# Moving three of the six h-splits one or two steps later in the gate groups of a fused attention and SwiGLU layer

## The reference, cut to what matters

```python
    x = x + jnp.concatenate([o_a, o_b], axis=-1) @ w_out[layer]
    h = rms_norm(x, norm_ffn[layer])
    x = x + (jax.nn.silu(h @ w_gate[layer]) * (h @ w_up[layer])) @ w_down[layer]
return rms_norm(x, norm_final)
```

## Time and profile before

| | |
|---|---|
| median of 3 runs | 2003.74 us |
| runs | 2003.70, 2003.74, 2005.03 us |
| the profiled execution | 2003.88 us |
| its span, first to last instruction | 2002.2 us |
| busy PE, DVE, ACT | 1973.2, 1626.9, 982.1 us |

### The profile page before, as it was taken

One profiled execution on the slowest core, in us unless ns is written; L12 is line 12 of the kernel. 1 busy time (PEld: TensorE's weight loads), 2 busy tenths in 40 slices (PEclk: granted clock), 3 DMA queues, 4 the chain that ended last, 5 costly groups with the idle time before them and its releaser, 6 DMA issues.

```text
span 2002.2 us, 33017 instructions
## 1 busy us (share of the span) xinstructions
PE 1973.2 (99%) x13586; PEld 1792.3 (90%) x13586; DVE 1626.9 (81%) x2314; ACT 982.1 (49%) x1510; POOL 13.3 (1%) x16
## 2 busy tenths in 40 slices
PE   8999999999999999999999999999999999999998
PEld 7898878777679999999999999999999888888886
DVE  6833577878979878988988988988988989889895
ACT  6212467768754585444444444444444433433343
POOL 0000000000000000000000000000000000000002
PEclk9999999999999999999999999999999999999999
DMA  7782222222145453545544544534536764664722
GB/s 256 213 246 63 74 66 67 58 59 59 32 158 189 148 163 98 173 148 165 172 148 152 186 138 150 197 130 155 194 131 222 277 230 154 245 216 163 252 85 84
DMA packets 211910, 306.20 MB, mean 153 GB/s; under 512 B 8752, under 2 KB 148144, under 8 KB 207152
## 3 DMA queue, kind: packets, MB, share of 16 engines
q1 hardware_dynamic: 211328, 303.50, 46.1%
q10 hardware_dynamic: 432, 0.59, 0.1%
HBM read 248.48 MB, written 55.57 MB: 152 GB/s over the span
## 4 chain that ended last, share of the span: by engine, by line
PE 95%; DVE 2%; ACT 1%; issue 1%; DMA 0%; DVEq 0%; ACTq 0%
PE bank L3107 13%; PE bank L3110 13%; PE bank L3112 13%; PE bank L3159 6%; PE bank L3162 6%; PE bank L3164 6%; PE bank L2826 3%; PE bank L2994 2%; PE bank L2998 2%; PE bank L2996 2%; PE bank L2893 2%; PE bank L2681 2%; PE bank L2682 2%; PE bank L2683 2%; PE bank L2853 2%; PE bank L2974 2%
## 5 line engine op out<-in xcount | busy, mean ns | idle before, releaser
L1516 ACT ACTIVATE w_all<-raw 128x1024 fp32r<-128x1024 f32 x292 | 307.1, 1062 | 310.2 <-PE bank L3164 156.9
L2281 DVE TENSOR_TENSOR w_all<-raw,w_all 128x1024 fp32r<-128x1024 f32 x292 | 353.3, 1221 | 56.9 <-ACT w_all L1516 56.3
L3107 PE MATMUL bank<-x_T,w_all 128*128 128x256 f32 x1344 | 370.9, 276 | 0.0
L3110 PE MATMUL bank<-x_T,w_all 128*128 128x256 f32 x1344 | 370.9, 276 | 0.0
L3112 PE MATMUL bank<-x_T,w_all 128*128 128x256 f32 x1344 | 370.9, 276 | 0.0
L3107 PE MATMUL bank<-x_B,w_all 128*128 128x256 f32 x1008 | 278.4, 276 | 0.8 <-ACT proj_q L1653 0.8
L3110 PE MATMUL bank<-x_B,w_all 128*128 128x256 f32 x1008 | 278.2, 276 | 0.0
L3112 PE MATMUL bank<-x_B,w_all 128*128 128x256 f32 x1008 | 278.2, 276 | 0.0
L1516 ACT ACTIVATE w_all<-proj_q 128x1024 fp32r<-128x1024 f32 x150 | 158.9, 1061 | 192.4 <-PE bank L3112 125.6
L3112 PEld LDWEIGHTS bank<-x_T,w_all 128*128 128x128 f32 x1344 | 252.3, 188 | 0.0
L3107 PEld LDWEIGHTS bank<-x_T,w_all 128*128 128x128 f32 x1344 | 252.3, 188 | 0.0
(11 more groups left out here) (342 smaller groups left out, 4311.0 us busy)
## 6 DMA issues: line engine op xcount, KB each, us to landing
raw<-in_w_gate SPq DMA_DIRECT2D x39, 1024.0 KB, 5.2
h_scratch<-late SPq DMA_DIRECT2D x70, 512.0 KB, 3.2
raw<-in_w_down SPq DMA_DIRECT2D x50, 512.0 KB, 5.1
proj_q<-in_w_up SPq DMA_DIRECT2D x22, 1024.0 KB, 6.8
raw<-in_w_up SPq DMA_DIRECT2D x22, 1024.0 KB, 8.1
x_B<-h_scratch SPq DMA_DIRECT2D x20, 1024.0 KB, 4.8
x_T<-h_scratch SPq DMA_DIRECT2D x15, 1024.0 KB, 7.6
proj_q<-in_w_down SPq DMA_DIRECT2D x30, 512.0 KB, 6.3
```

Of the source, the lines that this page charges most:

```text
L1516: nc.scalar.activation(piece_hi(p), piece_raw(n, k), ACT.Copy).then_inc(piece_hi_done, 1)
L2281: nc.vector.tensor_tensor(piece_lo(p), piece_raw(n, k), piece_hi(p).bitcast(F32), ALU.subtract).then_inc(piece_lo_done, 1)
L3107: nc.tensor.matmul(dst, wh[:, t, cs], x_lo(x)[:, cols], start=start and part == 0 and t == 0 and a == 0, stop=False, skip_group_check=True)
L3110: nc.tensor.matmul(dst, wl[:, t, cs], x_hi(x)[:, cols], start=False, stop=False, skip_group_check=True)
```

## The change

The six h-splits j = 1 to 6 of ACT followed the pieces k = 0, 2, 3, 4, 5, 7. Now they follow k = 0, 2, 3, 5, 6, 7: split 4 stands one piece later (and so behind `copy_p1` too, which belongs to step 5), split 5 one piece later, the others where they were.

```diff
                     if not up:
-                        if k in (0, 2, 3, 4, 5, 7):
-                            h_hi_of(ended, (0, 2, 3, 4, 5, 7).index(k) + 1)
+                        if k in (0, 2, 3, 5, 6, 7):
+                            h_hi_of(ended, (0, 2, 3, 5, 6, 7).index(k) + 1)
                         if k == 13:
                             silu_of(n, c22_made, 1, 1)
```

## The result

In the first measurement the changed kernel was slower: 2031.88 us median of 4 executions (2031.56 to 2033.08), against 2003.77 us (2003.70 to 2005.03) for the kernel before, a ratio of 1.0129 with a 95% interval of 1.0091 to 1.0166. Four executions of 2.3 to 4.0 ms, at a mean granted clock of 0.66 to 0.97, are left out of all counts; every other one has 0.997 to 0.999. I take the profile of the first measurement (2033.08 us) first.

A forecast was written before the change was run, and what follows sets the result against it. PE was taken to bound the gate and up stage; its stalls of 1.14 us in gate group 18 and 0.23 in gate group 2, together 1.37, came off 2003.74 us, giving 2002.4 us, range 2001.3 to 2004.1.

The forecast's parts named there:

- (1): ACT's copy and piece 5 no longer wait for the store: -1.14 us in gate group 18, -0.23 in gate group 2.
- (4): What is late next in gate group 18: piece 5's low part ends 0.4 us ahead of PE, the stall goes entirely.
- rival B: In gate group 18 the wait goes over to DVE's piece 5 if the store lands later: 2003.0 us; chance 0.08.
- The sum: The runs' median 2003.74 us less the 1.37 us of PE's stalls in gate groups 2 and 18: 2002.4 us.
- if a pair takes more than 76.16 us: A sign of being wrong: a gate and up group pair lasting longer than the ordinary 76.16 us.
- (2): Split 4 behind the copy and piece 5 on ACT: paid from 4.43 us of idle time, price 0.
- (3): Split 5 behind piece 6 on ACT: starts near 1044.3, 1.3 us to spare before DVE asks, price 0.
- Rival C: DVE is held by split 5 in each of ten gate groups: slower, 2014 us if 5 us late; chance 0.04.
- Rival A: The gain isn't there in timed runs, the 5.0 us store being one execution's chance: 2003.5 us; chance 0.16.
- The rule of the Trainium skill's page "DMA: Bandwidth & Descriptors": For each split's store: fixed 2.0 us plus bytes at 436 GB/s, 3.2 us; gain then about 0.2 to 0.4 us.
- the agreement of three runs and the profiled execution: Median 0.14 us under the profiled execution, two of three runs within 0.04: as if the same stalls came back in each.

The follow-up runs named there:

- e5: The changed kernel again beside the kernel before: 8 executions at 2002 to 2006 us, 3 at 2031 to 2034; median 2003.0 us against 2005.58.
- e13: The changed kernel again on one more chip: 6 executions at 2002 to 2006 us, 5 at 2031 to 2034; median 2004.30 us against 2004.09 before.
- e3: The changed kernel with DVE's low part of split 4 behind that of piece 5 in gate group 2: median 2002.57 us against 2009.22 before.
- e9: e3's kernel again on another chip, more executions: median 2003.81 us against 2003.94 for the kernel before, ratio 0.9991.
- e6: e3's kernel with idle DVE work in gate group 10, PE waiting about 0.1 us: 5 of 12 executions near 2020 to 2022 us.
- e14: e6's kernel again, a 0.1 us wait in gate group 10: 8 of 12 executions near 2020 to 2022 us.
- e1: The changed kernel with the old order in gate group 2, the new one in 4 to 20: 2002.5 to 2004.3 us seven times, 2032 twice.
- e11: e3's kernel with idle DVE work making PE wait about 0.7 us in gate group 10: 6 of 12 executions near 2020 to 2022 us.
- e12: e3's kernel with idle DVE work meant as a 1.0 us wait in gate group 10 (trace 1.2): 7 of 12 executions near 2020 to 2022 us.
- e2: The kernel before with the new order in gate group 2 alone: 2003.5 and 2003.9, 2009.2 and 2009.4, 2031.7 to 2031.9 us four times.
- e4: The kernel before with idle DVE work of various sizes ahead of piece 5's low part in gate groups 4 to 18: 2024.8 us, one execution.
- e7: e3's kernel with idle DVE work making PE wait about 0.5 us in gate group 10: 0 of 12 executions near 2020 to 2022 us.
- e8: e3's kernel with idle DVE work making PE wait about 1.5 us in gate group 10: 0 of 12 executions near 2020 to 2022 us.
- e10: The changed kernel, PE held about 1.6 us in gate group 4: 2003.9 to 2004.2 us four times, 2006.4, 2006.7, 2030.4 to 2031.4 five times, 2034.5.
- e15: e7's kernel again, a 0.5 us wait in gate group 10: 0 of 11 executions near 2020 to 2022 us.
- e16: e8's kernel again, a 1.5 us wait in gate group 10: 3 of 12 executions near 2020 to 2022 us.

## Why the prediction was wrong

**The step that failed** is the one on gate group 2 in (1): "In gate group 2 the shift is also over 4 us: -0.23." I looked for what is late next in gate group 18 only (4). Without the 0.23 us PE comes to piece 5 sooner by just that, and its low part isn't there: the wait went from piece 4 to piece 5. That is the place of my rival B, but in another group and by another cause, since DVE comes late there by its own work and not by split 4's store. Even at the quick pace the 0.23 us weren't gained: from the first piece of gate group 2 to that of 4 it takes 76.30 us in e5 and 76.28 in e13, against 76.39 before, a gain of 0.1. e3 shows this part: with that low part 0.6 us earlier by DVE's order the event is gone, and e3 and e9 have no execution above 2004.13 us.

**The assumption under it** failed as well, and it is where all of the 28 us lie: that PE loses at a wait what the wait lasts. The sum charges each wait its own length and puts nothing in for what PE does behind it. From gate group 2 on, an estimated 746 us of the stage are left at the quick pace; at 117.7 ns they take 3.9% more, 29 us (measured: the changed kernel's executions near 2032 us have a median of 2032.2, the others of 2002.7). From gate group 10 on it is 442 us and 17 (e6 and e14: 2020.1 and 2002.9), from gate group 18 on 138 us and 5.4 (the kernel before: 2009.5 and 2004.0). The classes are these places: the kernel before has events in gate groups 2 and 18 and shows 2032 and 2009, the changed one and e1 have none in 18 and never show 2009, e6 has its one in 10 and shows 2020, e3 has none. Only the one execution at 2017.0 us fits none of them. That a short wait can set the pace is shown most closely on one chip: no execution of 11 above 2004.2 us in e9 against 13 of 24 near 2021 in e11 and e12, which differ from it by the one wait. One sign that the prediction names for being wrong is the one that came, "if a pair takes more than 76.16 us": 28 pieces at the slow pace take an estimated 79.1.

**Point by point.** What (1) says of gate group 18 held: the copy's wait is gone, 2009 with it, and the pair takes 76.16 us in e5 and e13, the predicted 1.14 less. That executions at the quick pace gained 1.25 to 1.5 us, around the predicted 1.37, is in part luck: 1.14 and 0.1 come from the two places of the sum, the rest from elsewhere. (4) held too: in e5 piece 5's low part ends at 1427.86 in gate group 18 and its first matmul is due at 1428.20, 0.34 us later (I said 0.4). (2) and (3) held as well. ACT in gate group 8 of the changed kernel, from the copy to split 5, against the earlier trace rows, PE's first matmul of piece 4, and DVE at split 5:

```profile
1049.49 0.60 ACT L1653 ACTIVATE proj_q<-bank 128x512 f32<-128x512 f32 x1 [1.76 <-PE bank L3112]
1049.98 1.05 ACT L1516 ACTIVATE w_all<-raw 128x1024 fp32r<-128x1024 f32 x1
1051.82 0.64 ACT L1647 ACTIVATE late<-proj_q 128x512 fp32r<-128x512 f32 x1 [0.79 <-DMA h_scratch<-late]
1052.36 1.04 ACT L1516 ACTIVATE w_all<-raw 128x1024 fp32r<-128x1024 f32 x1
1053.56 0.63 ACT L1647 ACTIVATE late<-proj_q 128x512 fp32r<-128x512 f32 x1 [0.15 <-DMA h_scratch<-late]
...
1054.94 0.28 PE L3107 MATMUL bank<-x_B,w_all 128*128 128x256 f32 x1
...
1055.48 0.69 DVE L2424 TENSOR_TENSOR late<-proj_q,late 128x512 fp32r<-128x512 f32 x1
```

The copy ends 1054.94 - 1050.09 = 4.9 us ahead of its need (I said 4.6), split 4 waits 0.79 us for the store (1.2), and split 5 ends 1.3 us ahead of DVE's need, as worked out. Rival C didn't occur. Rival A, that the store of 5.0 us in gate group 18 was the chance of one execution, is settled by the other traces: it takes 5.0 us in e1, e3, e5, e9 and e13 too, and 5.1 in e2, which has the old order there and PE's wait with it:

```profile
1426.48 0.38 PE L3108 MATMUL bank<-x_B,w_all 128*128 128x256 f32 x1 [0.91 <-ACT proj_q L1653]
```

The rule of the Trainium skill's page "DMA: Bandwidth & Descriptors" that the prediction sets against it, an estimated 3.2 us, is fitted to transfers that GpSimd issues; SP issues these, so it could not decide the matter, and seven traces have 5.0 or 5.1. But the prediction read the agreement of three runs and the profiled execution as one steady time, and that was weak: the kernel before had 20 of 131 executions at 2032 us and 20 at 2009 to 2011, the first measurement included.

Whether the changed kernel is slower "by" its event is a matter of shares: 12 of 26 against 9 of 74 on the same chips. The counts say that its event sets the slow pace more often than that of before. Why, I can't say: the two differ in the piece, in what is late and by how much (in the traces PE's load comes 0.2 us late before, 0.1 after), but the share also differs from chip to chip for one kernel (10 of 25 against 1 of 32).

## What to carry to other kernels

Where the matrix engine is kept full by others that are just in time, removing one wait asks for the next thing to be late at every place that had a wait, not at the largest alone: two subtractions would have shown it. In the trace of before DVE's low part of piece 5 ends at 817.79 + 1.22 = 819.01 us. PE's last matmul of piece 3 starts at 816.23, so without its stall it would start piece 4 at 816.34 and load the weights of piece 5, 0.11 us ahead of its first matmul, at 816.34 + 2.72 - 0.11 = 818.95. It is the weight load that counts: the matmul itself is due at 819.06, when the low part is there.

```profile
816.23 0.28 PE L3112 MATMUL bank<-x_T,w_all 128*128 128x256 f32 x1
...
817.79 1.22 DVE L2281 TENSOR_TENSOR w_all<-proj_q,w_all 128x1024 fp32r<-128x1024 f32 x1
```

A short wait inside a long run of matmuls can cost far more than its length, so give each operand a few tenths of a microsecond to spare (e3 did so with one move, and stayed under 2004.2 us in 21 executions on two chips). And where the executions of one kernel fall into classes, count them on several chips ahead of reading a ratio: four against four said 1.3% here, where later sets said -0.2% and +0.4%.

## What the runs showed of the hardware

PE has two steady paces for the same stream of matmuls (128 x 256, each with its weight load; operands that ACT and DVE write as `fp32r`) at the same granted clock of 1.00: one every 113.3 ns or one every 117.7 ns. It holds either over hundreds of microseconds. In the four traces that change pace (the changed kernel's, e4, e6, e14) it changes at a matmul ahead of which PE waited, to the slow pace in all four and back in e4. A wait doesn't have to change it: in the traces of before, e1, e2, e5, e7, e8, e10, e11, e12, e13, e15 and e16 PE waited and the pace stayed quick.

The Trainium skill, "TensorE: Matmul & The Clock Gate", section "Back-to-back issue gap", gives N / 2.4 + 2.5 ns at the upper clock for an isolated matmul, an estimated 109.2 ns for 256 columns. For a stream with weight loads it says that both operations set the spacing, and gives about 81 ns for 128 columns and 131 for 512; both paces here lie between these. That the two paces are two ways in which loads and matmuls follow each other is a guess, which no run here tests.
